# Low parts of x on VectorE, a third column group ahead of a modulation tile's sum, and two row products at other steps

## The chip, the cores and the metric

The kernel runs on one core of one Trainium2 chip. The metric is the device time of one execution in microseconds (us): 1505.47 us, the median of three runs (1504.87 to 1506.13). The core has five engines with an instruction queue each: TensorE (PE; its weight loads are listed apart as PEld), VectorE (DVE), ScalarE (ACT), GpSimd (POOL) and SyncE (SP), which here issues the transfers of the weights.

## The reference, cut to what matters

The program is two transformer blocks on 256 tokens of width 1024, in float32. The change lies in the first one:

```
mod = silu(c) @ w_ada + b_ada                    # 1 x 6144
sh1, sc1, gt1, sh2, sc2, gt2 = split(mod, 6)
h = rms_norm(x, g_norm_mix) * (1 + sc1) + sh1
proj = h @ w_in                                  # q, k, v of two attentions, and f_logit
fox = forgetting_attention(q, k, v, cumsum(log_sigmoid(f_logit)))
sb = stick_breaking_attention(q, k, v)
x = x + gt1 * (concat(rms_norm(fox), rms_norm(sb)) @ w_out)
h2 = rms_norm(x, g_norm_ffn) * (1 + sc2) + sh2
x = x + gt2 * peer_layer(h2, ...)                # w_query, choice of experts, gathered rows
```

Each attention has 8 heads of 64. The value of x behind w_out is called x1 here. The peer layer multiplies h2 by w_query, chooses 16 experts for each of 8 heads and each token, and gathers their rows of two tables by index. The second block (another mixer and feed-forward layers) comes behind it and is not touched.

## The kernel before, in words

**Weights.** Every weight matrix comes in tiles of 2 MB, [128, 8, 512] (512 columns, all 1024 rows), into one of five buffers W[0] to W[4]. w_ada has twelve such tiles, ada[0] to ada[11], two to each sixth of mod; w_in has six, win[0] to win[5]; w_out two; w_query four. SyncE issues the loads in one fixed order: ada 0, 2, 1, the halves of win[0] and ada[3], win 1, win 2, ada 4, win 3, ada 5, win 4, ada 6, ada 7, win 5, ada 8, ada 9, w_out 0, ada 10, w_out 1, and then w_query. A load waits until the tile that lay in its buffer before has been used by TensorE, and the loads behind it in that order wait with it. The first tile of w_out lies in the buffer of ada[8], the second in another. "Fourth", "seventh", "eighth" and "ninth modulation tile" mean ada[3], ada[6], ada[7] and ada[8]; "sixth input tile" is win[5].

**Products.** A product of two float32 matrices is made in three products of fp32r parts: high by high, low by high, high by low (L1577, with L1573 and L1575 as the last instruction of a group). ScalarE casts the high part of a tile (WH, L1962), and VectorE subtracts it for the low part (WL, L2333), both in four pieces of [128, 2, 512]. x, scaled, shifted and turned, goes through the same: XH is its high part, cast by ScalarE for the first half of its rows and by VectorE (L2401) for the second, and XL its low part, subtracted by GpSimd (`put_x`, L2917). TensorE waits for both ahead of the columns that it reads:

```
pe.wait_ge(SE if k < 4 else VE, ("xh", k // 2))
pe.wait_ge(GE, ("xl", k // 2))
```

win[0] is worked through in four column groups (`first_part`), each in two halves of 12 matmuls over rows 0 to 3 and 4 to 7, because the scale of x's second half comes only with ada[3].

**Modulation.** c is one vector, so a tile of w_ada is multiplied by a column of silu(c) and summed over rows. VectorE does it for the later tiles: one multiplication (L2363) and then multiply-adds of [128, 512] (L2365), into LNV. TensorE sums LNV over the partitions with a product with a constant (L1560, `LNV,K`), and this frees the tile's buffer. `do.ada_rows(j, k0, n)` issues n such sums from row k0 on. `close_rows(j)` issues the product, marks the tile as used (with which the loads that waited for it are issued), and adds the result on VectorE (L2416):

```
def close_rows(j):
    u = bank()
    do.ada_rows_product(j, u)
    close_tile(ada[j])
    do.ada_rows_close(j, u)
```

**Order.** The program is written out by hand. `fm_tile` works through an input tile in four column groups and calls a hook behind each; `beside` is a list of what each call issues: sums of ada[5] to ada[7] (`row(j, k0, n)`), pieces of the split of win[4] and win[5] (`piece`), and products (`close`). win[5] (the values of forgetting attention) goes by token halves in `tm_tile`, with four calls of `fox_pass`: each takes two steps of forgetting attention (a step is the scores of one head, the transposition of an earlier one and the values of one before that), a step of `row_of_9` behind each (sums of ada[9]), and the next entry of a second list `beside`, the norm of stick-breaking attention's heads. The eight sums of ada[8] (`later_rows(8)`, four entries of two) go into a queue of things to do ahead of win[5]'s first half, and are taken there with `tick(4)`; `later_close(8)` is the next entry, and comes behind the first token half of win[5]. `bank()` deals out TensorE's result banks in turn, so each added or moved product also moves which bank the next ones get, and which earlier reader they wait for.

GpSimd's instructions near the start are the four subtractions of x, and behind them the zeroing of the buffers of q (`zero_q`, L2930, L2932).

Of the kernel before, what the change touches and what calls it, by code (L numbers as in the profile page):

```python
# [125 lines left out]
def build(nc, A, out, C1, C2):  # L126
    ctx = ExitStack()
    with ctx:
# [299 lines left out]
        def program(do):  # L428
# [199 lines left out]
            for c in range(0, 2):  # L628
                first_part(c, range(0, 4))
# [7 lines left out]
            for c in range(2, 4):  # L637
                first_part(c, range(0, 4))
# [108 lines left out]
            def piece(t):  # L747
# [3 lines left out]
            beside = [(row(5, 0, 4),), (row(5, 4, 2), piece(win[4])), (piece(win[4]), piece(win[4]), close(5)), (piece(win[4]), row(6, 0, 2)),  # L751
                      (row(6, 2, 4),), (row(7, 0, 2), close(6)), (row(7, 2, 4),), (piece(win[5]), piece(win[5]))]

            def beside_group():
                for step in beside.pop(0):
                    step()
                step_sb()

# [4 lines left out]
            for _ in range(2):  # L763
                split_piece(win[5])
            close_rows(7)
            do.note("fox in")
# [7 lines left out]
            later_rows(8)  # L774
            tick(4)
            later_close(8)
# [32 lines left out]
            beside = [(square,), (first, square1), (second, first1), (lambda: turned(at(6)), copy)]  # L809
# [12 lines left out]
            rows_9 = iter([None] * 2 + list(range(8)))  # L822
# [722 lines left out]
        def tensor(pe):  # L1545
# [16 lines left out]
            def dense(o, tile, pairs, ks, start, stop, names, parts=None, x=()):  # L1562
                for k in ks:
# [3 lines left out]
                    if parts:  # L1567
                        pe.wait_ge(SE if k < 4 else VE, ("xh", k // 2))
                        pe.wait_ge(GE, ("xl", k // 2))
# [110 lines left out]
            def forget_product(u):  # L1680
                for c in range(0, 8, 2):
                    pe.wait_ge(SE if c < 4 else VE, ("xh", c // 2))
                    pe.wait_ge(GE, ("xl", c // 2))
# [605 lines left out]
        def vector(dve):  # L2289
# [107 lines left out]
            def put_x(c, u):  # L2397
                v = pair(BIG[:, 6144 + c * 256:6656 + c * 256])
                if c >= 4:
                    dve.wait_ge(SE, ("x", c))  # L2400
                    e.tensor_copy(XH[:, c:c + 2, :], v).then_inc(*VE.up(("xh", c // 2)))  # L2401

# [497 lines left out]
        def gpsimd(pool):  # L2900
# [13 lines left out]
            def put_x(c, u):  # L2914
                v = pair(BIG[:, 6144 + c * 256:6656 + c * 256])
                pool.wait_ge(SE if c < 4 else VE, ("xh", c // 2))
                e.tensor_tensor(XL[:, c:c + 2, :], v, XH[:, c:c + 2, :].bitcast(F32), ALU.subtract).then_inc(*GE.up(("xl", c // 2)))  # L2917

# [70 lines left out]
            do.narrow_parts, do.put_x, do.zero_q, do.gather, do.rope_turn = narrow_parts, put_x, zero_q, gather, rope_turn  # L2989
# [167 lines left out]
```

## Time and profile before

| | us | share of the span |
|---|---|---|
| median of the runs | 1505.47 | |
| profiled execution, its own time | 1501.87 | |
| its span | 1500.1 | |
| TensorE busy | 1340.0 | 89% |
| VectorE busy | 1078.5 | 72% |
| ScalarE busy | 534.6 | 36% |
| GpSimd busy | 394.3 | 26% |

The core read 431.00 MB. The span is the time between the first and the last instruction of the profiled execution; its own time is what the runs' times are to be compared with. Busy shares are means over stages of different kinds: the first 180 us are the first mixer, then comes w_query, and from there to beyond 850 us the gathers of the experts. The chain of work that ended last is followed back from the last instruction, at each step to what released it.

### The profile page before, as it was taken

The numbers are of one execution on the slowest core, as the hardware profiler recorded it, in microseconds if no ns is written. First come the engines' busy times: TensorE is split into PE (matmuls) and PEld (weight loads), VectorE is DVE, ScalarE is ACT, GpSimd is POOL, SyncE is SP. The second block draws the span as 40 slices with busy tenths as digits, with TensorE's granted clock in tenths as the row PEclk, the third lists the DMA queues.
The fourth block names the chain that finished last, engine by engine and source line by source line (L and its number), as shares of the span: only waits on it lengthen the run. The fifth ranks groups of instructions, "written<-read, shape, count | busy, mean of one in ns | idle before, by whom it ended". The sixth has DMA issues, their size and how long they took to land.

```text
span 1500.1 us, 17348 instructions
## 1 busy us (share of the span) xinstructions
PE 1340.0 (89%) x6338; PEld 944.7 (63%) x6338; DVE 1078.5 (72%) x2034; ACT 534.6 (36%) x1040; POOL 394.3 (26%) x337
## 2 busy tenths in 40 slices
PE   6999989799998777777877799999999999999997
PEld 6887565356554323233323258879888788798896
DVE  6777789767897888888555576587656679876664
ACT  3453245422222212213211154535434355454440
POOL 1100034444444544454443202101101043011110
PEclk9999999999999999999999999999999999999999
DMA  9757589999999999999999994345554443455440
GB/s 364 281 200 265 183 342 394 402 421 416 420 421 406 421 421 421 422 410 406 408 422 422 402 333 151 113 146 194 179 211 172 172 158 123 148 203 210 169 169 28
DMA packets 116692, 433.17 MB, mean 289 GB/s; under 512 B 6896, under 2 KB 7152, under 8 KB 83584
## 3 DMA queue, kind: packets, MB, share of 16 engines
q0 software_dynamic: 36864, 268.45, 43.5%
q1 hardware_dynamic: 79456, 162.51, 30.5%
q8 instruction: 50, 0.82, 0.2%
q10 hardware_dynamic: 288, 1.11, 0.2%
q14 instruction: 34, 0.28, 0.1%
HBM read 431.00 MB, written 1.05 MB: 288 GB/s over the span
## 4 chain that ended last, share of the span: by engine, by line
PE 55%; DMA 21%; DVE 15%; ACT 5%; issue 2%; POOL 2%; SPq 0%; DVEq 0%; ACTq 0%; POOLq 0%
PE PS L1577 34%; DMA EB<-in_experts,EI 19%; PE PS L1804 4%; DVE EB L2666 4%; PE PS L1805 4%; PE PS L1560 3%; PE PS L1779 2%; PE PS L1573 1%; PE PS L1558 1%; DMA W<-in_w_out 1%; DVE WL L2333 1%; POOL EB L2945 1%; PE PS L1637 1%; PE PS L1819 1%; ACT BIG L2144 1%
## 5 line engine op out<-in xcount | busy, mean ns | idle before, releaser
L2945 POOL DMA_INDIRECT EB<-in_experts,EI x256 | 300.4, 1174 | 494.1 <-PE PS L1805 310.0
L2666 DVE CUSTOM_DVE_ANT_0 EB<-EB,Y 128x1024 f32<-128x1024 f32 x256 | 313.0, 1224 | 117.2 <-DMA EB<-in_experts,EI 116.5
L1804 PE MATMUL PS<-EB,BIG 128*128 128x512 f32 x512 | 279.0, 627 | 117.1 <-ACT BIG L2144 116.9
L2333 DVE TENSOR_TENSOR WL<-W,WH 128x1024 fp32r<-128x1024 f32 x216 | 279.8, 1344 | 88.6 <-ACT WH L1962 86.1
L1805 PE MATMUL PS<-EB,BIG 128*128 128x512 f32 x512 | 267.6, 605 | 0.0
L1804 PEld LDWEIGHTS PS<-EB,BIG 128*128 128x128 f32 x512 | 90.6, 195 | 252.4 <-ACT BIG L2144 182.6
L1962 ACT ACTIVATE WH<-W 128x1024 fp32r<-128x1024 f32 x216 | 213.4, 1048 | 71.3 <-PE PS L1573 67.6
L1577 PE MATMUL PS<-XH,WH 128*128 128x256 f32 x736 | 212.2, 288 | 0.6 <-ACT BIG L2188 0.6
L1577 PE MATMUL PS<-XL,WH 128*128 128x256 f32 x736 | 207.4, 282 | 0.0
L1577 PE MATMUL PS<-XH,WL 128*128 128x256 f32 x640 | 180.5, 282 | 0.0
L1805 PEld LDWEIGHTS PS<-EB,BIG 128*128 128x128 f32 x512 | 99.9, 195 | 127.2 <-issue 127.2
L2138 ACT ACTIVATE BIG<-BIG 128x2 f32<-128x2 f32 x128 | 26.0, 203 | 351.5 <-DVE BIG L2666 351.2
L1577 PEld LDWEIGHTS PS<-XH,WH 128*128 128x128 f32 x736 | 140.7, 191 | 2.7 <-issue 1.0
L1577 PEld LDWEIGHTS PS<-XL,WH 128*128 128x128 f32 x736 | 140.5, 191 | 1.4 <-issue 1.0
L2144 ACT ACTIVATE BIG<-K,BIG 128x128 f32<-128x128 f32 x256 | 88.8, 394 | 99.5 <-DVE BIG L2673 99.2
L1577 PEld LDWEIGHTS PS<-XH,WL 128*128 128x128 f32 x640 | 122.1, 191 | 0.0
L2960 POOL TENSOR_TENSOR AL<-Y,AH 128x512 fp32r<-128x512 f32 x28 | 36.3, 1298 | 299.1 <-DVE AH L2835 299.1
L1577 PE MATMUL PS<-WL,AH 128*128 128x512 f32 x256 | 101.5, 397 | 0.0
L1577 PE MATMUL PS<-WH,AH 128*128 128x512 f32 x256 | 100.9, 394 | 0.0
L1577 PE MATMUL PS<-WH,XH 128*128 128x512 f32 x224 | 92.9, 415 | 1.2 <-DVE XL L2341 0.7
L1577 PE MATMUL PS<-WL,XH 128*128 128x512 f32 x224 | 88.4, 395 | 0.0
L1577 PE MATMUL PS<-WH,AL 128*128 128x512 f32 x222 | 86.9, 391 | 0.0
(353 smaller groups left out, 1818.8 us busy)
## 6 DMA issues: line engine op xcount, KB each, us to landing
W<-in_ffn_w SPq DMA_DIRECT2D x32, 2048.0 KB, 8.8
W<-in_w_ada SPq DMA_DIRECT2D x11, 2048.0 KB, 10.6
W<-in_hy_w_in SPq DMA_DIRECT2D x6, 2048.0 KB, 11.4
W<-in_gla_w_in SPq DMA_DIRECT2D x6, 2048.0 KB, 8.1
W<-in_w_in SPq DMA_DIRECT2D x5, 2048.0 KB, 14.2
W<-in_w_out SPq DMA_DIRECT2D x2, 2048.0 KB, 13.4
W<-in_w_query SPq DMA_DIRECT2D x2, 2048.0 KB, 21.6
W<-in_w_query SPq DMA_DIRECT2D x4, 1024.0 KB, 6.8
```

Source lines behind the costliest of these rows:

```text
L1560: e.matmul(o, l, r, start=(i == 0), stop=True).then_inc(*TE.up(*names))
L1577: e.matmul(o, l, r, start=start and first, stop=False)
L1779: e.matmul(PS[u[0]][:, block(i)], w, x, start=k == 0, stop=False)
L1804: e.matmul(PS[u[0][0]][:, :], DG[i], rows_up[:, 1024:1536], start=start, stop=stop)
L1805: e.matmul(PS[u[1][0]][:, :], DG[i], rows_up[:, 1536:2048], start=start, stop=stop).then_inc(*TE.up(("up", s)))
L1962: e.activation(tile.hi[:, k, :], tile.w[:, k, :], ACT.Copy).then_inc(*SE.up(("hi", tile.index, n)))
L2138: e.activation(acts[:, g], dots[:, g], ACT.Gelu).then_inc(*SE.up(("gelu", s)))
L2144: e.activation(DG[s % NDG], ident, ACT.Copy, scale=acts[:, s:s + 1]).then_inc(*SE.up(("diagonal", s)))
L2333: e.tensor_tensor(tile.lo[:, k, :], tile.w[:, k, :], tile.hi[:, k, :].bitcast(F32), ALU.subtract).then_inc(*VE.up(("lo", tile.index, n)))
L2666: e.tensor_tensor_reduce(out=u, in0=u, in1=Y[:, s // 128, :], scale=1.0, scalar=0.0, op0=ALU.mult, op1=ALU.add, accum_out=dots[:, s:s + 1] ...
L2945: e.indirect_dma_start(out=EBUF[i], out_offset=None, in_=A["experts"][:, :], in_offset=bass.IndirectOffsetOnAxis(ap=EI[:, t, j:j + 1], axi ...
L2960: e.tensor_tensor(lo, r, hi.bitcast(F32), ALU.subtract).then_inc(*GE.up(("squares lo", *name[1:]), name))
```

## The change

It has three parts. First, the four subtractions of x's low parts go from GpSimd to VectorE: `put_x` of GpSimd goes, the one of VectorE makes both parts, and TensorE waits for VectorE where it waited for GpSimd. With it the third column group's first half over win[0] (`first_part(2, ...)`) is issued ahead of `ada_end(3, ...)`, TensorE's sum of the fourth modulation tile, where it stood behind. Second, in the first `beside` list the sums of ada[6] go as 3 and 3 instead of 2 and 4, those of ada[7] as 4 and 2 instead of 2 and 4, the product of ada[6] is issued behind the fifth call of the hook (`behind`) instead of in the sixth, one piece of win[5] is split in the seventh call, and behind the list one piece follows `close_rows(7)` where two stood ahead of it. Third, the eight sums of ada[8] stand in three places (2, 3 and 3) instead of one, its product (`close(8)`) in the third `fox_pass`, and the sums of ada[9] begin two steps later.

```diff
--- before.py
+++ after.py
@@ -625,7 +625,7 @@
             do.ada_close(2, 1, shift1)
             do.ada_sums(3, ada[3], range(0, 4))
             do.ada_sums(3, ada[3], range(4, 8))
-            for c in range(0, 2):
+            for c in range(0, 3):
                 first_part(c, range(0, 4))
             do.ada_end(3, ada[3], scale1)
             o.used.update(ada[j].index for j in range(4))
@@ -634,8 +634,7 @@
             do.ada_close(3, 3, scale1)
             do.scale_half(1)
             split_piece(win[0])
-            for c in range(2, 4):
-                first_part(c, range(0, 4))
+            first_part(3, range(0, 4))
             do.put_x(4, x_banks[4])
             do.put_x(6, x_banks[6])
 
@@ -748,21 +747,22 @@
                 return lambda: split_piece(t)
 
 
-            beside = [(row(5, 0, 4),), (row(5, 4, 2), piece(win[4])), (piece(win[4]), piece(win[4]), close(5)), (piece(win[4]), row(6, 0, 2)),
-                      (row(6, 2, 4),), (row(7, 0, 2), close(6)), (row(7, 2, 4),), (piece(win[5]), piece(win[5]))]
+            beside = [(row(5, 0, 4),), (row(5, 4, 2), piece(win[4])), (piece(win[4]), piece(win[4]), close(5)), (piece(win[4]), row(6, 0, 3)),
+                      (row(6, 3, 3),), (row(7, 0, 4),), (row(7, 4, 2), piece(win[5])), (piece(win[5]), piece(win[5]))]
+            behind = {4: close(6)}
 
             def beside_group():
                 for step in beside.pop(0):
                     step()
                 step_sb()
+                behind.get(7 - len(beside), lambda: None)()
 
             while o.behind:
                 tick()
             fm_tile(win[3], lambda u, c: do.put_q(win[3], c, u), hook=beside_group)
             fm_tile(win[4], lambda u, c: do.put_k("F", win[4], c, u), hook=beside_group)
-            for _ in range(2):
-                split_piece(win[5])
             close_rows(7)
+            split_piece(win[5])
             do.note("fox in")
             fox_u = at(4)
             fox = forgetting(0, fox_u)
@@ -771,9 +771,7 @@
             do.fetch_keys()
             while o.behind:
                 tick()
-            later_rows(8)
-            tick(4)
-            later_close(8)
+            do.ada_rows(8, 0, 2)
 
             def norm_of_heads(key, t, u):
 
@@ -806,7 +804,7 @@
 
             square, first, second, turned, copy = norm_of_heads("sb", 0, values["sb"][0])
             square1, first1, second1, turned1, copy1 = norm_of_heads("sb", 1, values["sb"][1])
-            beside = [(square,), (first, square1), (second, first1), (lambda: turned(at(6)), copy)]
+            beside = [(square, row(8, 2, 3)), (first, row(8, 5, 3), square1), (second, close(8), first1), (lambda: turned(at(6)), copy)]
 
             def fox_pass():
                 for _ in range(2):
@@ -819,7 +817,7 @@
                 do.put_tokens(VF[t], win[5], t, u)
                 do.note(("v fox", t))
 
-            rows_9 = iter([None] * 2 + list(range(8)))
+            rows_9 = iter([None] * 4 + list(range(8)))
 
             def row_of_9():
                 k = next(rows_9, None)
@@ -1566,7 +1564,7 @@
                     pe.wait_ge(VE, ("lo", tile.index, k // 2))
                     if parts:
                         pe.wait_ge(SE if k < 4 else VE, ("xh", k // 2))
-                        pe.wait_ge(GE, ("xl", k // 2))
+                        pe.wait_ge(VE, ("xl", k // 2))
                     for n, (l, r) in enumerate(pairs(k)):
                         first, end = k == ks[0] and n == 0, k == ks[-1] and n == 2
                         if end and names:
@@ -1680,7 +1678,7 @@
             def forget_product(u):
                 for c in range(0, 8, 2):
                     pe.wait_ge(SE if c < 4 else VE, ("xh", c // 2))
-                    pe.wait_ge(GE, ("xl", c // 2))
+                    pe.wait_ge(VE, ("xl", c // 2))
                 narrow(u, "wf", 8, (), ("forget",))
 
             def forget_logits(u):
@@ -2399,6 +2397,10 @@
                 if c >= 4:
                     dve.wait_ge(SE, ("x", c))
                     e.tensor_copy(XH[:, c:c + 2, :], v).then_inc(*VE.up(("xh", c // 2)))
+                    dve.wait_ge(VE, ("xh", c // 2))
+                else:
+                    dve.wait_ge(SE, ("xh", c // 2))
+                e.tensor_tensor(XL[:, c:c + 2, :], v, XH[:, c:c + 2, :].bitcast(F32), ALU.subtract).then_inc(*VE.up(("xl", c // 2)))
 
             def ada_rows(j, k0, n):
                 tile = ada[j]
@@ -2911,11 +2913,6 @@
                 pool.wait_ge(GE)
                 e.memset(lo.bitcast(F32), 0.0).then_inc(*GE.up(("narrow", key)))
 
-            def put_x(c, u):
-                v = pair(BIG[:, 6144 + c * 256:6656 + c * 256])
-                pool.wait_ge(SE if c < 4 else VE, ("xh", c // 2))
-                e.tensor_tensor(XL[:, c:c + 2, :], v, XH[:, c:c + 2, :].bitcast(F32), ALU.subtract).then_inc(*GE.up(("xl", c // 2)))
-
             def zero_q(kind, after):
                 Q = {"S": QS, "F": QF, "D": QD}[kind]
                 if after is None:
@@ -2986,7 +2983,7 @@
                 pool.wait_ge(GE)
                 e.tensor_tensor(o, o, gn.unsqueeze(1).broadcast_to([128, 2, 256]), ALU.mult).then_inc(*GE.up(("silu gain", j, t)))
 
-            do.narrow_parts, do.put_x, do.zero_q, do.gather, do.rope_turn = narrow_parts, put_x, zero_q, gather, rope_turn
+            do.narrow_parts, do.zero_q, do.gather, do.rope_turn = narrow_parts, zero_q, gather, rope_turn
             do.put_squares, do.zero_am, do.level_decays, do.silu_gain = put_squares, zero_am, level_decays, silu_gain
             return do
 
```

On VectorE, near the start, ahead of the fourth modulation tile's first row (`ada3a_landed` is the landing of its first half; `win0a` that of win[0]'s). Before:

```order
L2365 SCALAR_TENSOR_TENSOR LNV<-W,ST,LNV 128x512 [waits vector_done] x4
L2333 TENSOR_TENSOR WL<-W,WH 128x1024 [waits win0a_landed,scalar_done]
L2333 TENSOR_TENSOR WL<-W,WH 128x1024 [waits scalar_done]
L2380 TENSOR_TENSOR ST<-PS,ST 128x4 [waits vector_done,tensor_done]
L2382 TENSOR_TENSOR ST<-PS,ST 128x4 [waits vector_done]
L2363 TENSOR_SCALAR LNV<-W,ST 128x512 [waits vector_done,ada3a_landed]
```

and now:

```order
L2363 SCALAR_TENSOR_TENSOR LNV<-W,ST,LNV 128x512 [waits vector_done] x4
L2403 TENSOR_TENSOR XL<-BIG,XH 128x512 [waits scalar_done]
L2331 TENSOR_TENSOR WL<-W,WH 128x1024 [waits win0a_landed,scalar_done]
L2403 TENSOR_TENSOR XL<-BIG,XH 128x512 [waits scalar_done]
L2331 TENSOR_TENSOR WL<-W,WH 128x1024 [waits scalar_done]
L2378 TENSOR_TENSOR ST<-PS,ST 128x4 [waits vector_done,tensor_done]
L2380 TENSOR_TENSOR ST<-PS,ST 128x4 [waits vector_done]
L2361 TENSOR_SCALAR LNV<-W,ST 128x512 [waits vector_done,ada3a_landed]
```

Two subtractions of x's low part (XL) stand between the sums and the splits of win[0]; line numbers of VectorE's helpers are two lower.

On VectorE, at the ninth modulation tile, which lands in buffer 0 (`tile_landed_0`), behind the splits of win[5] (in buffer 2). L2416 or L2418 is the addition of the eighth tile's result, L2490 or L2492 the maximum of a head's scores, L2451 or L2453 the copy of value tokens. Before:

```order
L2333 TENSOR_TENSOR WL<-W,WH 128x1024 [waits tile_landed_2,scalar_done]
L2333 TENSOR_TENSOR WL<-W,WH 128x1024 [waits scalar_done] x3
L2416 TENSOR_TENSOR GV<-GV,PS 128x512 [waits vector_done,tensor_done]
L2363 TENSOR_SCALAR LNV<-W,ST 128x512 [waits vector_done,tile_landed_0]
L2365 SCALAR_TENSOR_TENSOR LNV<-W,ST,LNV 128x512 [waits vector_done] x7
L2490 TENSOR_REDUCE ST<-PS 128x1 [waits tensor_done] x2
L2518 COPY Y<-PS 128x512 [waits vector_done]
L2451 COPY BIG<-PS 128x512 [waits tensor_done]
```

and now:

```order
L2331 TENSOR_TENSOR WL<-W,WH 128x1024 [waits tile_landed_2,scalar_done]
L2487 TENSOR_TENSOR EB<-EB,PS 128x384 [waits vector_done,tensor_done]
L2331 TENSOR_TENSOR WL<-W,WH 128x1024 [waits scalar_done] x2
L2418 TENSOR_TENSOR GV<-GV,PS 128x512 [waits vector_done,tensor_done]
L2331 TENSOR_TENSOR WL<-W,WH 128x1024 [waits scalar_done]
L2361 TENSOR_SCALAR LNV<-W,ST 128x512 [waits vector_done,tile_landed_0]
L2363 SCALAR_TENSOR_TENSOR LNV<-W,ST,LNV 128x512 [waits vector_done]
L2492 TENSOR_REDUCE ST<-PS 128x1 [waits tensor_done] x2
L2520 COPY Y<-PS 128x512 [waits vector_done]
L2363 SCALAR_TENSOR_TENSOR LNV<-W,ST,LNV 128x512 [waits vector_done] x3
L2453 COPY BIG<-PS 128x512 [waits tensor_done]
```

The block of one multiplication and seven multiply-adds is broken up: two stand behind the last split, three behind the first two maxima (ahead of the copy of the value tokens), and three further down.

On TensorE, behind the first token half of win[5] (its last matmul is the first row): scores of a head (`MR`, `BIG`, `K,ST`), transposition (`K,EB`), values (`BIG,EB`). Before:

```order
L1573 MATMUL PS<-WH,XL 128x512
L1560 MATMUL PS<-LNV,K 128x512 [waits tile_landed_0,vector_done]
L1735 MATMUL PS<-MR 128x128 [waits vector_done]
L1736 MATMUL PS<-BIG 128x128
L1737 MATMUL PS<-K,ST 128x128
L1748 MATMUL PS<-K,EB 128x128 [waits scalar_done]
L1735 MATMUL PS<-MR 128x128 [waits scalar_done]
L1736 MATMUL PS<-BIG 128x128
L1737 MATMUL PS<-K,ST 128x128
L1748 MATMUL PS<-K,EB 128x128 [waits vector_done]
L1577 MATMUL PS<-WH,XH 128x512 [waits scalar_done]
```

and now, up to the same place:

```order
L1571 MATMUL PS<-WH,XL 128x512
L1733 MATMUL PS<-MR 128x128
L1734 MATMUL PS<-BIG 128x128
L1735 MATMUL PS<-K,ST 128x128
L1746 MATMUL PS<-K,EB 128x128 [waits vector_done,scalar_done]
L1733 MATMUL PS<-MR 128x128
L1734 MATMUL PS<-BIG 128x128
L1735 MATMUL PS<-K,ST 128x128
L1746 MATMUL PS<-K,EB 128x128 [waits scalar_done]
L1575 MATMUL PS<-WH,XH 128x512 [waits scalar_done]
```

and behind it, a half token half and a pass later:

```order
L1746 MATMUL PS<-K,EB 128x128 [waits scalar_done]
L1558 MATMUL PS<-BIG,EB 128x64
L1733 MATMUL PS<-MR 128x128 [waits scalar_done]
L1734 MATMUL PS<-BIG 128x128
L1735 MATMUL PS<-K,ST 128x128
L1746 MATMUL PS<-K,EB 128x128 [waits scalar_done]
L1558 MATMUL PS<-BIG,EB 128x64
L1558 MATMUL PS<-LNV,K 128x512 [waits vector_done,tile_landed_0]
L1575 MATMUL PS<-WH,XH 128x512
```

The ninth tile's product (`LNV,K`) stood behind the first token half; it now stands behind the third pass of forgetting attention, ahead of the last half token half. The first scores behind the token half have no wait of their own any more, the first transposition waits for VectorE as well.

## Rows read from the trace of the kernel before

**Rows 1.** Page, chain of work that ended last, share of the span by engine.

```profile
PE 55%; DMA 21%; DVE 15%; ACT 5%; issue 2%; POOL 2%; SPq 0%; DVEq 0%; ACTq 0%; POOLq 0%
```

**Rows 2.** Chain in order of time, 125 to 182 us: start, us, what.

```profile
142.49 18.32 DMA W<-in_w_out
...
160.86 1.99 PE PS L1637 x4
...
165.43 0.86 PE PS L1560 x2
...
173.20 0.70 DVE Y L2539
```

**Rows 3.** Timeline of SyncE, 100 to 160 us: start, us, instruction.

```profile
117.54 0.37 SPq L3003 DMA_DIRECT2D W<-in_w_in  x1
...
141.46 0.37 SPq L3003 DMA_DIRECT2D W<-in_w_out  x1
...
142.49 4.07 SPq L3003 DMA_DIRECT2D W<-in_w_out  x1
```

**Rows 4.** Timeline of GpSimd, 28 to 48 us.

```profile
45.52 1.28 POOL L2917 TENSOR_TENSOR XL<-BIG,XH 128x512 fp32r<-128x512 f32 x1 [0.36 <-DVE XH L2401]
```

**Rows 5.** Timeline of VectorE, in short windows between 28 and 45 us.

```profile
28.29 1.64 DVE L2365 SCALAR_TENSOR_TENSOR LNV<-W,ST,LNV 128x512 f32<-128x512 f32 x1
29.84 1.21 DVE L2333 TENSOR_TENSOR WL<-W,WH 128x1024 fp32r<-128x1024 f32 x1
...
31.16 2.10 DVE L2333 TENSOR_TENSOR WL<-W,WH 128x1024 fp32r<-128x1024 f32 x1
...
43.37 0.43 DVE L2401 CAST XH<-BIG 128x512 fp32r<-128x512 f32 x1
44.28 1.16 DVE L2401 CAST XH<-BIG 128x512 fp32r<-128x512 f32 x1 [0.49 <-ACT BIG L1986]
```

**Rows 6.** VectorE by lines, 120 to 181 us: busy us, mean ns, idle before.

```profile
L2365 DVE SCALAR_TENSOR_TENSOR LNV<-W,ST,LNV 128x512 f32<-128x512 f32 x23 | 17.3, 752 | 0.8
L2333 DVE TENSOR_TENSOR WL<-W,WH 128x1024 fp32r<-128x1024 f32 x4 | 4.6, 1220 | 3.1 <-ACT WH L1962 3.1
...
L2551 DVE TENSOR_TENSOR Y<-X,GV 128x512 f32<-128x512 f32 x2 | 1.4, 693 | 0.1
```

**Rows 7.** Chain in order of time, 38 to 50 us.

```profile
39.96 1.87 PE PS L1560 x8
41.82 2.56 PE PS L1577 x11
...
46.87 1.28 PE PS L1577 x11
```

**Rows 8.** Windows: length, busy of PE, PEld, DVE, ACT, POOL, PEclk, DMA, GB/s.

```profile
37.00:39.80 2.80, 0.00 (x0) 0.00 (x0) 2.69 (x4) 0.00 (x0) 0.00 (x0) 0.96 1.04 385
40.00:46.40 6.40, 6.40 (x30) 6.40 (x31) 4.78 (x8) 4.08 (x8) 2.16 (x2) 0.50 1.05 386
...
142.30:145.50 3.20, 3.20 (x14) 3.07 (x15) 2.77 (x7) 0.85 (x5) 0.00 (x0) 0.52 0.92 246
146.00:150.00 4.00, 4.00 (x26) 3.46 (x25) 2.23 (x6) 2.07 (x6) 0.00 (x0) 1.00 1.05 398
```

**Rows 9.** Timeline of TensorE, 133 to 151 us.

```profile
134.28 0.30 PE L1735 MATMUL PS<-MR 128*128 128x128 f32 x1 [1.15 <-DVE GV L2416]
...
135.39 0.48 PE L1577 MATMUL PS<-WH,XH 128*128 128x512 f32 x1
...
140.30 1.13 PE L1560 MATMUL PS<-LNV,K 128*128 128x512 f32 x2 [1.86 <-DVE LNV L2365]
142.02 0.47 PE L1735 MATMUL PS<-MR 128*128 128x128 f32 x1 [0.60 <-DVE BIG L2451]
...
147.81 0.22 PE L1735 MATMUL PS<-MR 128*128 128x128 f32 x1
...
149.71 0.48 PE L1577 MATMUL PS<-WH,XH 128*128 128x512 f32 x1
```

## The prediction, made before the changed kernel was run

> **What bounds the kernel now.** I first read the page's chain of work that ended last: TensorE holds 55% of the span, DMA 21%, VectorE 15% [rows 1]. The change touches only the first 165 us, so I then read that chain in order of time, to see which wait ends last at each edited place. By it TensorE holds the chain from about 40 us until the sixth input tile has landed. Then VectorE takes over (the splits of the sixth input tile, then the eight row sums of the ninth modulation tile), then a single load: the second w_out tile, 18.32 us from its issue at 142.49 to 160.81, and TensorE starts on it at 160.86 [rows 2]. Its predecessors in that stretch end on VectorE: TensorE waits 1.86 us for the ninth tile's last sum, and the product runs from 140.30 to 141.43 [rows 9].
>
> Next I read the DMA queue (SyncE). w_out's first tile goes into the ninth modulation tile's buffer, so it is issued at 141.46, right when that tile's product ends; the eleventh modulation tile and then, at 142.49, w_out's second tile follow in program order [rows 3]. That is the fact on which I argue: whatever moves the ninth tile's product moves TensorE's start at 160.86 by the same amount, unless TensorE itself comes later than the load. It does not: it works through w_out's first tile and is waiting when the second lands. From 160.86 on TensorE runs without a gap up to 173.2, where VectorE continues with x1 [rows 2], and everything behind (query, choice of experts, gathers) hangs on x1.
>
> **The change part by part.** All times are on the axis of the profiled execution of before, span 1500.1 us, 1501.87 us with what lies around it; the median of the shown runs is 1505.47 us, 3.6 above. I work out the difference on the trace and add it to the median.
>
> *x's low parts on VectorE, and the third group ahead of the sum.* GpSimd's four subtractions go; the last is 1.28 us [rows 4]. VectorE gets four of 128x512 with two SBUF inputs: 0.69 us each by the nearest form [rows 6]. Against that, VectorE's own work was stretched while GpSimd ran: a row sum 1.64 us where the mean is 0.75, a split 2.10 where it is 1.22 [rows 5, 6]. So the stretch from 28.29 to the end of the second split at 33.26 (4.97 us) becomes 0.75+0.69+1.22+0.69+1.22 = 4.57, and as the first split started 0.09 before the sum ahead of it had ended (29.84, against 28.29+1.64 [rows 5]) I take 4.4 for the five: 0.6 sooner. The fourth tile's product, at 39.96 [rows 7], follows 0.6 sooner, and with it x's last half.
>
> There the second gain lies: GpSimd's last low part ended at 45.52+1.28 = 46.80 [rows 4]. On VectorE it comes 0.6 sooner from the product, 0.6 from 1.28 against 0.69, and 0.7 because the copy of 1.16 us shrinks to about 0.43 (it is stretched as the others are) [rows 5]: 45.0. TensorE must be free by then. Before, two groups of 12 matmuls stood between the product and the second halves, at half clock (0.50 from 40.0 to 46.4, after a gap with no matmul from 37 to 39.8 [rows 8]): some 2.5 us each, the first 2.56 [rows 7]. One of them now runs in the gap, so TensorE is free at 41.2+2.6 = 43.8 and waits for the low parts. The first second half ended at 46.87+1.28 = 48.15; now its last 6 matmuls start at 45.0 and take 0.7 us at full and 1.3 at half clock, so it ends 1.85 to 2.45 sooner. I take 2.0, nearer to half clock, as the row of that stretch has it. Bounds: 1.2 (the clock stays down longer) and 2.8. From 48 to 127 TensorE is the chain, so this arrives whole. GpSimd's zeroing of Q moves up into its idle time; the change of GpSimd's set-up that stood before its first subtraction goes to a later one that waits for TensorE: nothing.
>
> The Trainium skill (SBUF — State Buffer, Who interferes with whom) says that a VectorE instruction with two SBUF inputs and a GpSimd instruction that reads SBUF shut each other out for a whole instruction. By that, VectorE could have lost up to four GpSimd durations, 5.1 us at 1.28; the trace has about 0.9 us in each stretched instruction, and the sum goes by the rows.
>
> *Seventh product a step sooner.* It moves ahead of one group of 24 matmuls (about 2.9 us), so the sixth input tile's load leaves at 114.7 instead of 117.54 [rows 3]. One of its splits then fits ahead of the last group, and only one is left behind the eighth tile's product. Price: that tile's four sums now stand before a head's logs on VectorE, 1.3 us, which by my count leaves TensorE 0.1 to 0.2 us of wait. Gain: the wait of 1.15 us at 134.28 [rows 9], before the first scores, is gone: they start at 133.3, 1.0 sooner. Bounds: 0 and 1.2.
>
> *Ninth tile's rows spread, and its product a pass later.* The block of eight sums is broken up, and TensorE's 1.86 us wait before 140.30 goes. But the product no longer follows the first token half: it stands behind the second pass of forgetting attention, half a tile of products and the third pass. From 133.3: pass 1.1 us (134.28 to 135.39), half a tile 2.85 (135.39 to the wait before 140.30, which began at 138.44, less the last matmul's drain of some 0.2), pass 1.3, half a tile 2.85, pass 1.9 (147.81 to 149.71) [rows 9], a product of two matmuls 0.86 at full clock (165.43 [rows 2]): 144.1. A new wait comes on top: with the banks dealt out anew, the first transposition waits for VectorE's copy of the value tokens (before, the third scores waited 0.60 for it, at 142.02 [rows 9]), and in VectorE's order three sums of 0.78 us stand ahead of that copy. Counted from the last split, which I put at 133.1, two sums (1.3), two maxima (0.55), a copy (0.7), three sums (2.4) and that copy (0.7) with gaps of 0.2 end at 138.95; TensorE arrives at 137.8. So it waits 1.15 us, and I add 0.2 for ScalarE behind it. So the product ends at 145.5 instead of 141.43: 4.05 later. Bounds: 3.0 (no new wait) and 5.0.
>
> *Sum up to w_out.* The three loads leave 4.05 - 2.0 = 2.05 us later, and the second w_out tile lands at 162.9. Nothing else uses the engines then, so they take as long as before.
>
> *TensorE's clock behind that wait.* TensorE reaches the second w_out tile some 7 us ahead of its landing (about 155.5, w_out's first half done), where before it waited less than 1 us. After gaps of 3 us (37 to 40) and of about 2 us around 140.30 the granted clock was 0.50 for 6.4 us and 0.52 from 142.3 to 145.5, then 1.00 [rows 8]. A gap of 7 us is longer than either, so I expect half clock for 3.4 to 6 us behind the landing, where TensorE is the chain: half of that is lost, 1.7 to 3; I take 2.2. This carries to x1.
>
> The Trainium skill (TensorE: Matmul & The Clock Gate, HAM oscillation — how this bites in real kernels) describes just this: a wait for a transfer lets the clock fall, and the burst behind starts slow. The shorter gaps of this trace agree; no run here shows one of 7 us at this place.
>
> Forecast: 2.05 + 2.2 = 4.25 us slower, 1505.47 + 4.25 = 1509.7 us.
>
> **The rivals.**
> 1. *No clock loss, or a larger early gain.* If the clock holds behind the wait, or the early part gives 2.8 and more, the sum is 1 to 2.9 us: 1507.4. For it: clock and gaps do not fall in step in every execution. Against it: both longer gaps cost the clock.
> 2. *The later part swallows it.* The gathers move most of the bytes, and DMA is 21% of the chain; if their start had slack, the end would not move: 1505.5. Against it: no gather can leave before x1.
> 3. *Faster: w_out's load is not the end.* If the second tile were there when TensorE comes, the early 2.0, the 1.15 at 134.28, the 1.86 at 140.30 and the half-clock loss of 1.6 at 142.3 to 145.5 would all stay won: 6.6 sooner, 1498.9. It decides from the point where the ninth tile's product ends before 141.43; that needs the early part to give 4.05, twice what I find.
> 4. *The early part gives little* (VectorE's added 2.8 us fall on the path): +4.05 + 2.2 = 6.3, 1511.8.
>
> **How the numbers follow.** About 0.2% (3 us) is what a measurement of this kernel can tell from no change. Chances: forecast 0.50 (with its own range of +2.9 to +5.7, 1508.4 to 1511.2), rival 1 0.22, rival 2 0.06, rival 3 0.13, rival 4 0.09. Slower by over 0.2%: the forecast but for 0.03 of it, and rival 4, 0.56; within: that 0.03 and rivals 1 and 2, 0.31; faster: rival 3, 0.13. The range leaves out rival 3 and the far end of rival 4: 1504.5 to 1512.0.
>
> **What would show it.** Right: no subtraction on GpSimd before 100 us; the first second half ends near 46; the sixth input tile's load leaves near 112.7 (114.7 less 2.0); w_out's first load leaves near 143.5 and its second tile lands near 162.9; TensorE idles some 7 us before it, and the granted clock is about 0.5 behind it; x1 is 4 us later. Wrong: if w_out's first load leaves before 141.4, or if TensorE is not waiting when it lands; then rival 3 holds. If the clock stays 1.00 from 163 on, the last term falls.

## The result

The changed kernel takes 1509.02 us (median of 7 runs, 1508.12 to 1511.23) against 1504.87 us (7 runs, 1503.46 to 1506.13) of the kernel before: ratio 1.0032, 95% interval 1.0022 to 1.0042. It is 4.15 us slower by the medians, 4.8 us by the ratio. The forecast was 4.25 us slower, 1509.7 us.

### The profile after

Its profiled execution has a span of 1507.2 us. The chain by engine has hardly moved (TensorE 56%, DMA 20%, VectorE 15%), so the page alone would not tell where the time went; the places of the prediction do. All times are on the axis of each kernel's own span, which begins with the same rows of SyncE in both.

The first place is x's second half. The chain in order of time of the changed kernel (start, us, what):

```profile
41.89 0.44 DVE XH L2399
...
42.35 0.69 DVE XL L2403
...
44.26 0.82 PE PS L1575 x5
45.08 0.12 PE PS L1571
45.20 1.29 PE PS L1575 x11
```

VectorE's cast and subtraction follow each other (XH, XL), and the last low part ends at 43.41 + 0.69 = 44.10. The first second half ends at 45.08 + 0.12 = 45.20, where it ended at 46.87 + 1.28 and one more matmul of 0.12 = 48.27 before [rows 7]: 3.1 us sooner. The eleven matmuls ahead of the last one of a second half take 1.29 us, as they did at full clock before (1.28 from 46.87 [rows 7]).

The second place is where the seventh modulation tile's product went. TensorE's timeline, with the idle time and its releaser in brackets:

```profile
109.60 1.98 PE L1556 MATMUL PS<-W,ST 128*128 128x512 f32 x4 [0.59 <-DVE LNV L2363]
...
116.05 0.70 PE L1700 MATMUL PS<-BIG 128*128 128x256 f32 x2 [0.79 <-DVE BIG L2448]
```

Both waits are new. At 109.60 the seventh tile's sums are not ready. At 116.05 TensorE waits for VectorE's copy of the previous column group before the next scores; in the kernel before, the product stood just there. The chain of before, same place:

```profile
114.93 1.72 PE PS L1558 x4
116.65 0.86 PE PS L1560 x2
117.51 0.43 PE PS L1702 x2
```

The two products (1.72 and 0.86 us) covered that copy; the scores of L1702 followed them without a gap and took 0.43 us, where they take 0.70 us behind the new wait.

The third place is the ninth modulation tile. TensorE after:

```profile
132.01 0.30 PE L1733 MATMUL PS<-MR 128*128 128x128 f32 x1
...
137.52 0.30 PE L1746 MATMUL PS<-K,EB 128*128 128x128 f32 x1 [0.81 <-DVE BIG L2453]
...
143.16 1.08 PE L1558 MATMUL PS<-LNV,K 128*128 128x512 f32 x2
...
163.29 3.78 PE L1635 MATMUL PS<-W,XT 128*128 128x512 f32 x4 [7.14 <-DMA W<-in_w_out]
```

The first scores come at 132.01 without a wait (134.28 with one of 1.15 before [rows 9]). The first transposition waits 0.81 us for VectorE's copy of the value tokens, and the product ends at 143.16 + 1.08 = 144.24 (141.43 before). SyncE's issues and the chain behind them:

```profile
112.47 0.37 SPq L3000 DMA_DIRECT2D W<-in_w_in  x1
...
144.27 0.37 SPq L3000 DMA_DIRECT2D W<-in_w_out  x1
...
145.30 3.65 SPq L3000 DMA_DIRECT2D W<-in_w_out  x1
```

```profile
145.30 17.95 DMA W<-in_w_out
...
163.29 3.78 PE PS L1635 x4
...
170.65 0.86 PE PS L1558 x2
...
178.42 0.70 DVE Y L2541
```

The sixth input tile's load leaves 5.1 us sooner than before, w_out's loads 2.8 us later [rows 3]. The second w_out tile lands at 163.25 (160.81 before), TensorE has waited 7.14 us for it, and the four matmuls that follow take 3.78 us where they took 1.99 [rows 2]. The granted clock of these stretches (columns as in rows 8):

```profile
156.00:163.20 7.20, 0.16 (x1) 0.00 (x0) 3.25 (x10) 1.02 (x3) 0.00 (x0) 0.69 1.05 387
163.30:167.50 4.20, 4.20 (x7) 2.03 (x8) 0.00 (x0) 0.00 (x0) 0.00 (x0) 0.50 1.05 385
167.50:170.00 2.50, 2.50 (x7) 1.23 (x6) 1.89 (x3) 0.00 (x0) 0.00 (x0) 0.71 0.11 36
170.20:178.40 8.20, 8.20 (x24) 3.90 (x22) 5.77 (x8) 1.41 (x3) 0.00 (x0) 1.00 0.00 0
```

TensorE is idle, then busy all the time at 0.50, which is 1.2 GHz, and back at 1.00 from 170.2. x1's step (L2541, in before L2539) starts at 178.42, 5.2 us later than before [rows 2]. The last gather of the experts' rows, in the kernel before and in the changed one:

```profile
851.22 0.94 POOL L2945 DMA_INDIRECT EB<-in_experts,EI  x1 [0.78 <-PE PS L1805]
```

```profile
855.87 0.94 POOL L2942 DMA_INDIRECT EB<-in_experts,EI  x1 [0.78 <-PE PS L1803]
```

It leaves 4.65 us later: x1's delay passes through the gathers nearly whole.

### The profile page after: what moved, and what is told of

It is laid out like the page before. It is cut to its first block, busy times and chain, and to the rows that moved or that the text cites. A ratio compares the mean times of both kernels' runs of the same rounds, so it can differ in the third digit from the quotient of the medians.

```text
span 1507.2 us, 17348 instructions
## 1 busy us (share of the span) xinstructions
PE 1343.1 (89%) x6338; PEld 944.0 (63%) x6338; DVE 1078.7 (72%) x2038; ACT 535.2 (36%) x1040; POOL 389.8 (26%) x333
## 3 DMA queue, kind: packets, MB, share of 16 engines
HBM read 431.00 MB, written 1.05 MB: 287 GB/s over the span
## 4 chain that ended last, share of the span: by engine, by line
PE 56%; DMA 20%; DVE 15%; ACT 5%; issue 2%; POOL 1%; SPq 0%; DVEq 0%; ACTq 0%; POOLq 0%
PE PS L1575 33%; DMA EB<-in_experts,EI 18%; PE PS L1802 5%; PE PS L1803 4%; DVE EB L2668 4%; PE PS L1558 3%; PE PS L1777 2%; PE PS L1571 1%; DVE WL L2331 1%; PE PS L1556 1%; DMA W<-in_w_out 1%; PE PS L1635 1%; DVE LNV L2363 1%; PE PS L1817 1%; ACT BIG L2142 1%
```

## The experiments

Each was timed in five rounds against the kernel before on the same chip.

### The three parts alone

First part:

```diff
-            for c in range(0, 2):
+            for c in range(0, 3):
                 first_part(c, range(0, 4))
...
+                e.tensor_tensor(XL[:, c:c + 2, :], v, XH[:, c:c + 2, :].bitcast(F32), ALU.subtract).then_inc(*VE.up(("xl", c // 2)))
```

> The first part alone on the kernel before: x's low parts on VectorE and the third column group ahead of the fourth modulation tile's sum. Theory (the first half of the prediction, as the changed kernel's trace shows it): the first second half over the first input tile ends 3 us sooner than before, everything up to w_out's loads and x1 shifts by these 3 us, and the time is 3 us below before, 1501.9 against 1504.9. Rival 4 (VectorE's added subtractions land on the path later): no gain, within 1 us of before. Rival 2 (the gathers swallow what x1 gains): x1 3 us sooner in the trace and the time as before.

Measured: 1501.32 against 1503.94 us, ratio 0.9981 (0.9971 to 0.9992), 2.9 us faster. w_out's second load leaves at 140.02 (142.49 before), TensorE waits 0.7 us for it, and x1's step starts at 170.14, 3.1 us sooner:

```profile
140.02 17.74 DMA W<-in_w_out
...
157.80 1.98 PE PS L1636 x4
...
170.14 0.70 DVE Y L2542
```

The early gain arrives whole at x1 and at the end. Rivals 2 and 4 of the prediction fall: nothing later swallows what x1 gains, and VectorE's added work does not come back.

Second part:

```diff
+                      (row(6, 3, 3),), (row(7, 0, 4),), (row(7, 4, 2), piece(win[5])), (piece(win[5]), piece(win[5]))]
+            behind = {4: close(6)}
```

> The second part alone: the seventh modulation tile's product a step sooner, its sums and the eighth's dealt otherwise, the sixth input tile's pieces earlier. The prediction gave it a gain of 1.0 us up to the first scores of forgetting attention. The changed kernel's trace shows two waits of TensorE that before has not, 0.59 us ahead of that product (its last sum) and 0.79 us ahead of the scores behind the next column group (VectorE's copy of the keys, which the product stood in front of before). Theory now: these 1.4 us and a slower product eat the 1.15 us that goes at the first scores: the first scores come 0 to 0.8 us later than before, the time is 0 to 1 us above before. Rival (the prediction's term holds): 1 us below before.

Measured: 1504.19 against 1503.94 us, ratio 1.0004 (0.9995 to 1.0013): no change. The same two waits are there, 0.60 and 0.78 us:

```profile
112.47 1.98 PE L1559 MATMUL PS<-W,ST 128*128 128x512 f32 x4 [0.60 <-DVE LNV L2366]
...
118.90 0.70 PE L1703 MATMUL PS<-BIG 128*128 128x256 f32 x2 [0.78 <-DVE BIG L2447]
```

x1's step starts at 173.44, 0.2 us later than before. What the part gains at the first scores it has lost ahead of them; the prediction's gain of 1.0 us for this part does not exist.

Third part:

```diff
-            later_rows(8)
-            tick(4)
-            later_close(8)
+            do.ada_rows(8, 0, 2)
...
+            beside = [(square, row(8, 2, 3)), (first, row(8, 5, 3), square1), (second, close(8), first1), (lambda: turned(at(6)), copy)]
```

> The third part alone: the ninth modulation tile's sums spread over three places and its product a pass later. Theory: the product ends 5.1 us later than before (12.2 us behind the first scores where it was 7.2), w_out's loads leave 5.1 us later, TensorE waits some 7.5 us for the second tile and has half its clock behind it (2.8 us, as in the changed kernel): x1 7 to 8 us later, the time 1512 to 1513. Rival (w_out's load is not the end, TensorE gains what the block of sums cost): 3 us below before. Rival without the clock: 5 us above before.

Measured: 1511.95 against 1503.94 us, ratio 1.005 (1.0036 to 1.0063), 7.5 us slower. x1's step starts at 179.63, 6.4 us later:

```profile
147.69 17.67 DMA W<-in_w_out
...
165.41 3.78 PE PS L1635 x4
...
179.63 0.70 DVE Y L2537
```

```profile
PE PS L1635 <- DMA W<-in_w_out: 6.9, 1, 6.9
```

w_out's second load leaves 5.2 us later, as expected, and the time is in the expected 7 to 8 us above before, but x1's 6.4 us lie below the 7 to 8 expected for it: the load itself is 0.65 us shorter, which brings the wait to 6.9 us, and the half clock behind the landing is over sooner than in the changed kernel:

```profile
165.40:169.20 3.80, 3.79 (x6) 1.62 (x7) 0.00 (x0) 0.00 (x0) 0.00 (x0) 0.50 1.05 387
169.20:171.50 2.30, 2.30 (x11) 1.29 (x11) 1.60 (x3) 0.00 (x0) 0.00 (x0) 0.99 0.39 134
```

From the landing (165.36) to x1's step are 14.3 us, 1.9 us more than before; in the changed kernel it is 2.8 us more. By the ratios the three parts add up: -2.9 + 0.6 + 7.5 = 5.2 us, against 4.8 for the whole change. At x1's step of the profiled executions they do so less well (-3.1 + 0.2 + 6.4 = 3.5 us, against 5.2): 0.7 us of the difference are there when the second tile lands, 0.9 us are the half clock. All of the loss is the third part, and it is larger than the whole.

### Is it the load's order?

```diff
-        wout.append(plan(A["w_out"], 0, 0, 0))
+        wout.append(plan(A["w_out"], 0, 512, 1))
+        wout.insert(0, plan(A["w_out"], 0, 0, 0))
         plan_ada(10, 4)
         ada[10].load_after = ((TE, ("used", win[4].index)),)
-        wout.append(plan(A["w_out"], 0, 512, 1))
```

On the changed kernel:

> The changed kernel with one line moved: w_out's second tile is loaded ahead of its first, since its buffer comes free with the fifth input tile (126 us), long before the ninth modulation tile's product. Theory (the order of the loads makes that product the bound): the wait of 7.1 us for the second tile and the half clock behind it go; TensorE is then held only by VectorE's chain of the heads' norm (its last scaling ended at 160.7 in the changed kernel, TensorE would want it at 158.1): x1 comes 8 to 9 us sooner than in the changed kernel, 3 to 4 us sooner than before, the time is 1501 to 1502. Rival 2 (x1 does not set the end): as the changed kernel, 1509.

Measured: 1500.73 against 1503.94 us, ratio 0.998 (0.9971 to 0.9989): 3.0 us faster than before, 0.52% below the changed kernel by the two ratios (0.998 / 1.0032). w_out's second tile is issued at 129.72; SyncE then stands in the same row (two loads) until 144.71; the product that frees the first tile's buffer ends at 143.24 + 1.08 = 144.32. TensorE goes from the first tile to the second without a wait for a load (156.05), and waits only for VectorE's last scaling:

```profile
129.72 14.99 SPq L3000 DMA_DIRECT2D W<-in_w_out  x2
144.76 0.58 SPq L3000 DMA_DIRECT2D W<-in_w_ada  x1
```

```profile
156.05 1.88 PE L1635 MATMUL PS<-W,XT 128*128 128x512 f32 x4
159.50 0.66 PE L1618 MATMUL PS<-K,Y 128*128 128x128 f32 x4 [1.57 <-DVE Y L2531]
```

x1's step starts at 170.07, 8.35 us sooner than in the changed kernel. With the same sums, the same late product and one line of the loads' plan moved, the loss is a gain. On the kernel before:

> The kernel before with w_out's second tile loaded ahead of its first, and nothing else. Theory (in the kernel before TensorE and the second tile arrive together, within 0.1 us, so the load's order costs it nothing, and it is the change that makes the load the bound): no wait for w_out, x1 within 0.5 us of before, the time within 1 us of before. Rival (the load order held the kernel before as well): 2 us or more below before.

Measured: 1503.87 against 1505.12 us, ratio 0.9996 (0.9987 to 1.0005), no change; x1's step is at 173.53 (173.20 before). TensorE does not wait for w_out there. In the kernel before TensorE and the load arrived together, so the order cost nothing.

### The clock behind the wait

```diff
+                if (j, t, half, ks[0]) == (1, 0, 0, 0):
+                    freed(u)
+                    for n in range(14):
+                        k = n % 4
+                        e.matmul(PS[u[0]][:, :], XT[:, k, block(t)], wout[0].w[:, k, :], start=n == 0, stop=n == 13)
                 pe.wait_ge(TILE[tile.s], ("tile", tile.index))
```

> The changed kernel with fourteen more matmuls (128x128 by 128x512, products of w_out's first tile whose result is overwritten) issued by TensorE in its wait for w_out's second tile, so that it is idle for about 1 us instead of 7.1 ahead of it; the load lands when it did. Theory (the half clock behind the wait is a cost of its own): the granted clock behind 163.3 is 1.00 instead of 0.50, the four matmuls there take 2.0 us instead of 3.78, x1 comes 2.6 us sooner than in the changed kernel and the time is 1506.4 against 1509.0. Rival (the clock is down for another reason than the idle engine, such as the loads that run at the same time): 0.50 still, x1 at 178.4, the time as in the changed kernel.

Measured: 1510.87 against 1504.75 us, ratio 1.0044 (1.003 to 1.0058), a miss in its size: each matmul stands as two rows and takes 0.87 us, so the fourteen ran for 12.2 us and ended at 167.9, 4.6 us past the landing of the changed kernel (163.3). It tells of the clock alone (1.00 in every window from 150 to 180 us), not of the time. With eight (`range(8)`):

> The same as the run with fourteen more matmuls, with eight: each took 0.87 us there (two rows of 0.43 in the trace), so the fourteen ran 4.6 us past the landing. Eight take 7 us and end at 162.9, ahead of the landing at 163.3. Theory (the half clock behind the wait is a cost of its own): granted clock 1.00 behind 163.3, the four matmuls there take 1.9 instead of 3.78 us, x1 2.6 us sooner than in the changed kernel, the time 1506.4 against 1509.0. Rival (x1's later start is swallowed): trace as said, the time as in the changed kernel.

Measured: 1508.34 against 1505.12 us, ratio 1.0018 (1.0009 to 1.0027), against 1.0032 (1.0022 to 1.0042) of the changed kernel: 2.1 us less by the ratios, with intervals that overlap a little, where 2.6 were expected: the time alone does not settle it. The trace does:

```profile
156.08 7.03 PE L1627 MATMUL PS<-W,XT 128*128 128x512 f32 x16
164.18 1.98 PE L1640 MATMUL PS<-W,XT 128*128 128x512 f32 x4 [1.08 <-DMA W<-in_w_out]
```

```profile
156.00:163.20 7.20, 7.11 (x17) 2.85 (x15) 3.27 (x11) 1.02 (x3) 0.00 (x0) 1.00 1.05 386
...
163.30:167.50 4.20, 3.32 (x11) 1.83 (x12) 0.75 (x1) 0.00 (x0) 0.00 (x0) 1.00 1.05 388
167.50:170.00 2.50, 2.50 (x10) 1.26 (x9) 1.58 (x3) 0.69 (x1) 0.00 (x0) 1.00 0.10 36
```

```profile
145.32 18.82 DMA W<-in_w_out
...
176.53 0.70 DVE Y L2546
```

TensorE is busy in the wait, the clock is 1.00 behind it, and the same four matmuls take 1.98 us. The load landed at 145.32 + 18.82 = 164.14 in that execution, 0.9 us later than in the changed kernel; from there to x1's step at 176.53 are 12.4 us, as before, against 15.2 us in the changed kernel. So 2.8 us of the changed kernel's loss at x1 are the clock in that execution (1.9 us in the one of the third part alone), and the idle TensorE is what takes it down: the loads beside it moved the same (387 and 386 GB/s up to the landing).

### The two edits of the first part

```diff
-            for c in range(0, 2):
+            for c in range(0, 3):
                 first_part(c, range(0, 4))
```

> The kernel before with only the third column group ahead of the fourth modulation tile's sum; x's low parts stay on GpSimd. Theory (the two edits of the first part need each other): GpSimd's last low part ends at 46.8 as before, so TensorE, free at 42 to 43, waits for it; the first second half ends at 47.5 to 48.2 against 48.15 before, 0 to 0.7 us sooner, and the time is 0 to 0.7 us below before. Rival (the gap was the whole gain): 2 us or more sooner, the time 2 us or more below before.

Measured: 1505.41 against 1504.75 us, ratio 1.0004 (0.9995 to 1.0013): no change, as expected. TensorE comes sooner and waits for GpSimd, and behind that wait the clock is down that the filled gap had kept up:

```profile
44.75 0.55 PE L1576 MATMUL PS<-XH,WH 128*128 128x256 f32 x1 [1.97 <-POOL XL L2916]
```

```profile
39.40:42.00 2.60, 1.87 (x16) 1.87 (x17) 2.46 (x5) 0.23 (x1) 0.00 (x0) 1.00 1.05 387
...
44.50:46.40 1.90, 1.62 (x6) 1.39 (x7) 1.63 (x3) 1.71 (x2) 1.41 (x3) 0.50 1.05 388
```

The low parts on VectorE alone (the third group stays behind the sum):

> The kernel before with only x's low parts on VectorE; the third column group stays behind the fourth modulation tile's sum. Theory: the low parts are there at 45 us, but TensorE comes out of the gap of 37 to 39.3 with half its clock as before and is at the two groups behind the product until 46; the first second half ends at 47.4 to 47.6 against 48.15, 0.6 us sooner, and the time is 0.6 us below before. Rival (VectorE's subtractions are the whole gain): 3 us sooner, the time 3 us below before.

Measured: 1502.83 against 1504.75 us, ratio 0.9986 (0.9977 to 0.9995), 2.1 us faster, between the expected 0.6 and the rival's 3. TensorE's half clock behind the gap is over by 44.5, where the kernel before still ran at 0.50 until 46.4 [rows 8], and the first second half ends 2.1 us sooner than before; why the half clock is over sooner is not shown:

```profile
42.00:44.50 2.50, 2.50 (x16) 2.50 (x16) 2.32 (x6) 2.50 (x6) 0.00 (x0) 0.66 1.05 386
44.50:46.40 1.90, 1.90 (x19) 1.90 (x17) 1.90 (x2) 1.00 (x2) 0.00 (x0) 1.00 1.05 389
```

w_out's load leaves at 139.44, 2.0 us sooner. x1's step at 172.34 is only 0.9 us sooner in the profiled execution, where the half clock behind the ninth tile's product lasted until 146 (0.50 from 142 to 146; before, 0.52 to 145.5 [rows 8]); whether it is so long in the timed runs is not shown. By the medians VectorE's subtractions give about 2 of the 3 us, and the third group nothing alone and the rest with them; the intervals of this run and of the whole first part overlap, so this split is a reading, not a measurement.

### A version that beats both

The first and third part, the exchanged loads, and the tenth modulation tile's product behind w_out's first output half:

> A version made from the findings: the first part and the third part of the change, without the second; w_out's second tile loaded ahead of its first; and the last sums of the tenth modulation tile behind the heads' norm on VectorE, with that tile's product behind w_out's first output half. Theory: against the version with the loads exchanged alone (x1 3.1 us sooner than before) the first scores come 0.6 us sooner, since the second part's waits are gone, and TensorE's wait of 1.6 us for VectorE's last scaling goes: x1 5 us sooner than before, 1499 us. Rival (VectorE is the bound of that stretch, so moved sums come back as another wait): 3 us below before, 1501.

Measured: 1500.38 against 1504.75 us, ratio 0.9976 (0.9966 to 0.9986), 3.6 us faster than before. x1's step starts at 169.48, 3.7 us sooner than before and not 5: TensorE still waits 1.6 us for VectorE's last scaling, since four of the sums were issued in the loop over forgetting attention's last steps and stood where they had stood. With `pass` in that loop and the sums behind `copy1()`:

> The version made from the findings, mended: there the four sums of the tenth modulation tile still stood ahead of the heads' norm (150.93 to 154.04) and TensorE waited 1.57 us for VectorE's last scaling; here they stand behind it. Theory: that wait goes, x1 (second output half) comes 1.6 us sooner than there and 5.3 us sooner than before, the time is 1498.8 against 1500.4 there. Rival (the sums come back as a later wait of TensorE or VectorE): as there, 1500.4.

Measured: 1501.71 against 1505.12 us, ratio 0.9981 (0.9971 to 0.9991). The wait is gone, but x1 and the time gain nothing by it, as the rival said:

```profile
158.40 3.12 DVE L2362 SCALAR_TENSOR_TENSOR LNV<-W,ST,LNV 128x512 f32<-128x512 f32 x4
...
162.15 2.32 DVE L2362 SCALAR_TENSOR_TENSOR LNV<-W,ST,LNV 128x512 f32<-128x512 f32 x3
...
169.19 0.69 DVE L2540 TENSOR_TENSOR Y<-PS,GV 128x512 f32<-128x512 f32 x1
```

The four sums (3.12 us) now stand ahead of the additions for x1, whose second step starts at 169.19 (169.48 in the version before this one). VectorE is the bound of that stretch: its timeline shows no wait from 157.61 to 169.88. The intervals of these versions and of the exchanged loads alone overlap, so the runs do not rank them; all three beat both kernels (the changed one by the ratios to the kernel before).

## Why the prediction was right

Its central step held: w_out's loads hang on the ninth tile's product, and moving it a pass later makes TensorE wait. The third part alone and the exchanged loads show it from both sides. That the sum came out within 0.6 us is partly luck, since two of its terms were wrong by more, in opposite directions. By steps:

- *First part.* Mis-sized, in the good direction: 3.1 us for 2.0, beyond the upper bound of 2.8. The term took the stretch behind the gap at nearly half clock; with the third group in the gap the clock stayed at 1.00, the product's row took 1.05 us (1.87 before [rows 7]), the last low part was there at 44.10 instead of 45.0, and the matmuls behind it ran at full clock.
- *Seventh product.* The step that failed. The prediction counted 1.0 us of gain at the first scores, which is there (the lead over before grows from 1.13 to 2.27 us between the last column group and those scores), and 0.1 to 0.2 us of wait, which were 0.59 us at the product's new place. It put at nothing what the product covered where it stood, VectorE's copy: 0.79 us of wait there. With 0.5 us of longer rows right behind the two waits (1.98 for 1.72, 0.70 for 0.43) that is 1.9 us; the second part alone measures as no change.
- *Ninth product.* 12.2 us behind the first scores were predicted, 12.24 measured (132.01 to 144.25), the new wait at the transposition 0.81 us for 1.15. Three loads leave 2.8 us later for 2.05, since the first two errors leave 0.8 us between them.
- *The load.* Second tile at 163.25 for 162.9, TensorE's wait 7.1 us for "some 7". The load took 17.95 us instead of the 18.32 that the prediction kept from before, and so hid half of the 0.8 us.
- *The clock.* 15.2 us from the landing to x1's step for 12.4 before: 2.8 us for 2.2, within its bounds of 1.7 to 3. The half clock lasted to 167.5 and part of the 2.5 us behind it. The price of such a wait is not one number: the third part alone had a wait nearly as long (6.9 us) and paid 1.9 us. Of rival 1's two conditions the first did not come about (the clock fell), the second did (the early part gave 3.1 us, more than 2.8); its time did not follow, since the seventh product took 1.9 us back. The rule of the Trainium skill (TensorE: Matmul & The Clock Gate, section HAM oscillation — how this bites in real kernels) that a wait for a transfer makes the burst behind it start slow, which no run showed at this place when the prediction was made, is shown by this wait (0.50 behind it) and by the run that filled it (1.00).
- *The sum.* x1's step is 5.2 us later in the trace for 4.25 predicted, the time 4.15 to 4.8 us. The profiled executions differ by 7.1 us in span. Of that, 4.65 us are there at the last gather; the rest comes behind it in stages that the change does not touch (a load of the second block leaves 4.6 us later at 943.83, the next row of that queue 5.9 us later at 985.07). The profiled execution of the kernel before is a quick one, 1501.87 us where the median is 1504.87, that of the changed kernel is its median; so the 7.1 us are no measure of the change. The match in the last digits of the forecast is that luck: 1.1 us too little on one side and 1.9 on the other.

Rival 3 (faster, the load is not the end) has its mechanism right and its condition wrong: once the second tile's load does not hang on the late product, TensorE starts on that tile at 156.05, 4.8 us sooner than before, where the rival listed 6.6; 1.57 us of it go to the wait for VectorE's last scaling, and 3.1 us are left at x1 and 3.0 us in the time.

## What to carry to other kernels

When a product also frees a buffer, its place on the engine is an issue time for a transfer: follow the buffer to the load, and all loads queued behind it, before moving the product for its own engine's sake. Before moving work away from a place, look at what it covers there: the instruction behind it may have an operand that is only just ready. A load that has its own free buffer should not stand in the queue behind one that waits; it pays only where that load is the bound, as the same exchange on the kernel before, without effect, shows.

## What the runs showed of the hardware

VectorE's subtractions of 128x512 took 0.68 to 0.69 us each, where GpSimd's took 1.28 to 1.93 us, and with GpSimd gone VectorE's own cast next to them went from 1.16 [rows 5] to 0.42 us and the split from 2.05 to 1.23. GpSimd's and VectorE's rows in the kernel before:

```profile
30.26 1.93 POOL L2917 TENSOR_TENSOR XL<-BIG,XH 128x512 fp32r<-128x512 f32 x1 [0.88 <-ACT XH L1990]
43.88 1.28 POOL L2917 TENSOR_TENSOR XL<-BIG,XH 128x512 fp32r<-128x512 f32 x1 [11.69 <-DVE XH L2401]
45.84 2.05 DVE L2333 TENSOR_TENSOR WL<-W,WH 128x1024 fp32r<-128x1024 f32 x1 [0.26 <-ACT WH L1962]
```

The two splits that met a subtraction (31.16 and 45.84) both end 1.1 us behind its end (32.19 and 46.80 [rows 4, 5]), and an undisturbed split takes 1.22 us [rows 6]; the cast at 44.28 ends 0.3 us behind the subtraction's end at 45.16, and an undisturbed one takes 0.43 us [rows 5]. So by these rows VectorE's instruction lasted until GpSimd's was done and then a little less than its own length: the 0.9 us that the prediction read as a stretch are what was left of GpSimd's instruction.

The granted clock of a short window and the length of the rows in it need not agree near the start: in the kernel before the window from 31.9 to 36.0 has a granted clock of 1.00, and all but one of the matmuls of 128x256 that begin in it last 0.41 to 0.42 us, as they do at 42 to 46, where the window has 0.50, and not the 0.28 us of the stretch from 46.7 on. In the run with the low parts alone the same window has 0.50, with matmuls of the same 0.41 to 0.42 us. Durations are the safer witness there.
